# A state-space layer on chunks of four frames, with its matrices and tables built during the first MLP

## The reference, cut to what matters

```python
def s5_grouped(u, ...):          # 128 groups of 16 channels, 64 complex states in each
    step = exp(log_step)[:, None]
    lam_bar = exp(lam * step)
    b_bar = ((lam_bar - 1.0) / lam)[:, :, None] * b
    bu = einsum('blgh,gph->blgp', uf, b_bar)
    _, h = associative_scan(combine, (lam_bar, bu), axis=1)   # h_t = lam_bar * h_{t-1} + bu_t
    y = real(einsum('blgp,ghp->blgh', h, c)) + d_skip * uf
...
    y = s5_grouped(rmsnorm(x, mix_norm_o), ...)
    val, gate = split(gelu(y) @ w_glu)
    x = x + val * sigmoid(gate)
    x = x + square(relu(rmsnorm(x, ffn_norm[1]) @ w_up[1])) @ w_down[1]
```

## Time and profile before

| | |
|---|---|
| median of three runs | 2263.25 us (2261.49 to 2263.97) |
| profiled execution, first to last instruction | 2258.3 us |
| between the two | 4.95 us |
| busy share PE / DVE / ACT / POOL | 92% / 67% / 43% / 36% |
| mean granted TensorE clock | 0.952 |
| state-space stage | about 1090 to 1342 us |
| first MLP | about 370 to 1090 us |

### The profile page before, as it was taken

How to read it: one execution, slowest core, us unless ns; L and a number is a source line. 1 busy time by engine, 2 the same in 40 slices (tenths; PEclk the granted TensorE clock), 3 DMA queues, 4 the chain that set the end, 5 groups by cost and what they waited for, 6 DMA issues and landing times.

```text
span 2258.3 us, 38008 instructions
## 1 busy us (share of the span) xinstructions
PE 2073.3 (92%) x12259; PEld 1774.8 (79%) x12259; DVE 1513.1 (67%) x1828; ACT 971.4 (43%) x1347; POOL 814.3 (36%) x1249
## 2 busy tenths in 40 slices
PE   6969699999999999999565569999999999999998
PEld 5758588888888888888444458888888888888887
DVE  6887777755665665656799975657656655655653
ACT  3425544444444444434423324444444444444443
POOL 4187765777767777102366650100000000000000
PEclk9979899999999999999776779999999999999999
DMA  8534356666666666676211116565555555655653
GB/s 199 160 113 136 109 182 200 192 206 198 191 205 197 195 201 198 190 223 207 79 38 33 37 36 186 174 197 181 189 186 182 185 191 179 186 191 179 185 193 131
DMA packets 388147, 374.86 MB, mean 166 GB/s; under 512 B 34667, under 2 KB 385276, under 8 KB 387836
## 3 DMA queue, kind: packets, MB, share of 16 engines
q1 hardware_dynamic: 384796, 363.51, 51.9%
q0 software_dynamic: 3104, 10.49, 1.5%
q10 hardware_dynamic: 192, 0.14, 0.0%
HBM read 361.38 MB, written 12.58 MB: 166 GB/s over the span
## 4 chain that ended last, share of the span: by engine, by line
PE 81%; DVE 13%; issue 3%; ACT 1%; SPq 1%; DMA 1%; DVEq 1%; POOL 0%; ACTq 0%
PE ps L514 53%; PE ps L516 26%; DVE gb L1502 3%; DVE ab L1492 1%; DVE Wl L1103 1%; DVE ctm L1477 1%; DVE A L1133 1%; DVE uc L1456 1%; DVE A L1522 1%; DVE du L1468 1%; ACT Wh L817 1%; SPq L446 0%; DVE us L329 0%; PE px L586 0%; DMA xin<-in_x_dram 0%
## 5 line engine op out<-in xcount | busy, mean ns | idle before, releaser
L514 PE MATMUL ps<-A,Wh 128*128 128x512 f32 x5280 | 1857.2, 401 | 27.9 <-DVE A L1412 19.1
L516 PE MATMUL ps<-A,Wl 128*128 128x256 f32 x5280 | 1432.8, 282 | 0.0
L1103 DVE TENSOR_TENSOR Wl<-raw,Wh 128x1024 fp32r<-128x1024 f32 x660 | 828.5, 1268 | 579.2 <-ACT Wh L817 570.6
L514 PEld LDWEIGHTS ps<-A,Wh 128*128 128x128 f32 x5280 | 975.7, 189 | 248.3 <-issue 22.1
L817 ACT ACTIVATE Wh<-raw 128x1024 fp32r<-128x1024 f32 x660 | 689.6, 1057 | 808.4 <-PE ps L516 503.3
L516 PEld LDWEIGHTS ps<-A,Wl 128*128 128x128 f32 x5280 | 1001.5, 190 | 32.2
L1601 POOL TENSOR_TENSOR sq<-xT 128x512 f32 (+1 forms) x32 | 40.4, 1264 | 359.6 <-DVE xT L1181 177.4
L742 PE MATMUL ps<-hb,cst 128*32 128x128 f32 x128 | 36.7, 384 | 99.5 <-POOL hb L1723 99.5
L1665 POOL TENSOR_TENSOR ttmp<-ctab 128x4 f32<-128x4 f32 (+6 forms) x224 | 120.5, 538 | 17.6
L1666 POOL TENSOR_TENSOR ctab<-ttmp 128x2 f32<-128x2 f32 (+6 forms) x224 | 119.5, 534 | 17.6
L963 ACT ACTIVATE A<-cross 128x512 f32 (+1 forms) x64 | 40.4, 632 | 197.7 <-DVE cross L1427 197.7
(11 more groups left out here) (260 smaller groups left out, 1247.2 us busy)
## 6 DMA issues: line engine op xcount, KB each, us to landing
raw<-in_w_up_dram SPq DMA_DIRECT2D x256, 512.0 KB, 3.9
raw<-in_w_down_dram SPq DMA_DIRECT2D x256, 512.0 KB, 3.4
raw<-in_w_glu_dram SPq DMA_DIRECT2D x64, 512.0 KB, 3.9
raw<-in_w_in_e_dram SPq DMA_DIRECT2D x52, 512.0 KB, 3.9
raw<-in_w_out_e_dram SPq DMA_DIRECT2D x32, 512.0 KB, 3.6
s_tables<-ctab POOLq DMA_DIRECT2D x32, 256.0 KB, 3.3
tab<-s_tables SPq DMA_DIRECT2D x32, 256.0 KB, 3.0
xin<-in_x_dram SPq DMA_DIRECT2D x2, 1024.0 KB, 6.4
```

The costliest lines, as they stand in the source:

```text
L514: wide = lambda: mm(ps[:, b + t, :], Wh[:, s, c, cols], A[:, k, :], start=(n == 0), stop=(n == KC - 1))
L516: half = lambda: mm(ps[:, b + t, 0:L], Wl[:, s, c, cols], A[:, k, 0:L], start=False, stop=False)
L1103: tt(Wl[:, s], raw[:, s], Wh[:, s].bitcast(F32), ALU.subtract).then_inc(lo_split, 1)
```

## The change

The state-space stage takes four frames at a time (`CT = 4`, `NC4 = 64` steps). For that each chunk needs larger matrices, which are now built in the two middle quarters of the first MLP, one chunk for every two pairs, by all engines together, are stored to memory as one block of 1 MB per chunk (`par_d`: input matrices, output matrices, direct matrices, cosines, sines and negated sines), and read back into four slots.

In the preparation PE, after each even pair of the two quarters, brings C and B into place (`s5_c_columns`, 4 matrix multiplications, `s5_b_rows`, 16), and after each odd pair forms the direct kernels (`s5_kernels`, 16); POOL forms the products with powers of `lam` and the tables, chunk by chunk; ACT and DVE copy from PSUM beside their weight splits. The two quarters and the stage are unrolled. POOL no longer makes `bbar` or tables anywhere else; the B and C matrices are loaded from the POOL queue after the first layer's mixer.

In the stage the input is scaled and put into memory by ACT during the last eight pairs (`u_d`) and read back with four frames on the partitions by POOL's queue; PE makes 16 small matrix multiplications for a chunk's scan input and 40 for its output, all of 64 x 64 tiles with 64 columns; DVE makes two products, one scan of 512 columns (decay, result in PSUM; a zero decay at each of the 8 segments' starts) and two products; POOL makes one subtraction for the turn, the input's scaling by the norm and the low part of the result; ACT fills the decay into PSUM, makes the gelu and the high part. The result goes through memory (`y_d`) to come back channel-major, by SP. The frames lie in another order within a chunk through the GLU, and the residual addition puts them back.

SP's program:

```diff
-            for k, s5_b in enumerate((s5_b_re, s5_b_im)):
-                sp.dma_start(braw[:, k], s5_b[0].rearrange("(j g) p h -> (g p) j h", g=2)).then_inc(b_loaded, 16)
...
-            sp.wait_ge(bbar_stored, 32)
-            sp.dma_start(bch[:, :, :], bbar_d.rearrange("c p f -> p c f")).then_inc(bc_loaded, 16)
-            for k, s5_c in enumerate((s5_c_re, s5_c_im)):
...
-            sp.wait_ge(tab_stored, KC * 32)
-            for c in range(2):
-                load_tables(c, c)
...
+            def load_slot(c):
+
+                if c >= NSLOT:
+                    sp.wait_ge(s5_y, c - NSLOT + 1)
+                sp.dma_start(slot[:, c % NSLOT, :], par_d[c]).then_inc(slot_loaded[c % NSLOT], 16)
+
+            sp.wait_ge(kd_stored, 16)
+            for j in range(2, 8):
+                load_pair(g + 8 + j, w_down[0], (QTR - 1) * D, j * TW)
+                if j - 2 < NSLOT:
+                    load_slot(j - 2)
...
+            for c in range(KC):
+                sp.wait_ge(s5_ge, c + 1)
+                sp.dma_start(y_d[c].rearrange("(t q) (j n) -> (q j) t n", t=TPC, j=CT), yb[:, c % 2])\
+                    .then_inc(y_stored[c % 2], 16)
+                if c + NSLOT < KC:
+                    load_slot(c + NSLOT)
+                sp.wait_ge(y_stored[c % 2], 16 * (c // 2 + 1))
+                if c >= 3:
+                    sp.wait_ge(a2_ready, 48 + c - 2)
+                sp.dma_start(yt[:, c % 3, :], y_d[c]).then_inc(y_loaded[c % 3], 16)
```

PE in the first MLP, then in the stage (`s5_out` waits for `s5_p` of its chunk):

```diff
+                if hook:
+                    for q in range(1, QTR - 1):
+                        for j in range(8):
+                            up(j, j % 2, q, False)
+                            hook((q - 1) * 16 + j)
+                        for j in range(8):
+                            down(j, j % 2, q)
+                            hook((q - 1) * 16 + 8 + j)
...
+            def s5_b_rows(c):
+
+                pe.wait_ge(bp_ready, c + 1)
...
+            def prepare(n):
+
+                if n % 2 == 0:
+                    s5_c_columns(n // 2)
+                    s5_b_rows(n // 2)
+                else:
+                    s5_kernels(n // 2)
...
+            s5_in(0)
+            s5_in(1)
+            for c in range(KC):
+                s5_out(c)
+                if c + 2 < KC:
+                    s5_in(c + 2)
```

DVE in the stage:

```diff
+            def s5_rotate(c):
+
+                dve.wait_ge(s5_v, c + 1)
+                if c >= 2:
+                    dve.wait_ge(s5_z, c - 1)
+                tt(ab[:, c % 2, 0], v_bank(c), cos_of(c), ALU.mult)
+                tt(ab[:, c % 2, 1], v_bank(c), sin_of(c), ALU.mult).then_inc(s5_rot, 1)
+
+            def s5_scan(c):
+
+                dve.wait_ge(s5_z, c + 1)
+                dve.wait_ge(s5_rho, c + 1)
+                nc.vector.tensor_tensor_scan(ps[:, 2 + c % 2, :], ps[:, c % 2, :], zb[:, c % 2].rearrange("p t k n -> p (t k n)"),
+                                             0.0, ALU.mult, ALU.add).then_inc(s5_g, 1)
...
+                tt(pp[:, c % 2, 0, :, :, 1:NC4 + 1], g_bank(c), cos_of(c), ALU.mult)
+                tt(pp[:, c % 2, 1, :, :, 1:NC4 + 1], g_bank(c), sin_of(c), ALU.mult).then_inc(s5_p, 1)
+
+            s5_rotate(0)
+            dve.wait_ge(pp_zero, 1)
+            for c in range(KC):
+                if c + 1 < KC:
+                    s5_rotate(c + 1)
+                s5_scan(c)
```

POOL in the first MLP:

```diff
+            def turns(c):
...
+                while n < NC4:
...
+                    link(tt(tmp[0][:, :, 0:n], c0, ct_, ALU.mult))
+                    link(tt(tmp[1][:, :, 0:n], s0, st_, ALU.mult))
+                    link(tt(tmp[2][:, :, 0:n], s0, ct_, ALU.mult))
+                    link(tt(tmp[3][:, :, 0:n], c0, st_, ALU.mult))
+                    tt(cos[:, :, n:2 * n], tmp[0][:, :, 0:n], tmp[1][:, :, 0:n], ALU.subtract)
+                    link(tt(sin[:, :, 0, n:2 * n], tmp[2][:, :, 0:n], tmp[3][:, :, 0:n], ALU.add))
+                    n *= 2
...
+            for c in range(KC):
+                b_powers(c)
+                turns(c)
+                c_powers(c)
+                store(c)
```

More of the change, by code:

```diff
@@ L767, in _, with s5_in @@
-            s5_prepare(0, 0)
-            s5_direct(0, 0)
-            s5_prepare(1, 1)
+            mlp(P_MLP0, 8, 2, 16, 2, hook=prepare)
+            def s5_in(c):
+                pe.wait_ge(us_ready, c + 1)
+                pe.wait_ge(slot_loaded[c % NSLOT], 16 * (c // NSLOT + 1))
+                if c >= 2:
+                    pe.wait_ge(s5_rot, c - 1)
+                for t in range(TPC):
+                    for k in range(2):
+                        for g in range(2):
+                            own = slice(64 * g, 64 * g + 64)
+                            n = S_IN + (2 * t + k) * HD
+                            last = mm(v_bank(c)[own, t, k, :], slot[own, c % NSLOT, n:n + HD], us2[own, c % 4, t, :],
+                                      start=True, stop=True)
+                last.then_inc(s5_v, 1)
@@ new lines, in s5_out @@
+            def s5_out(c):
+                pe.wait_ge(s5_p, c + 1)
+                if c >= 2:
+                    pe.wait_ge(s5_ge, c - 1)
+                direct = slot[:, c % NSLOT, S_DIR:S_COS].rearrange("p (t n) -> p t n", t=TPC)
+                for t in range(TPC):
+                    for g in range(2):
+                        own = slice(64 * g, 64 * g + 64)
+                        mm(y_bank(c)[own, t, :], direct[own, t], us2[own, c % 4, t, :], start=True, stop=False)
+                    for k, w, m in ((0, 0, 0), (0, 1, 1), (1, 1, 0), (1, 0, 1)):
+                        for g in range(2):
+                            own = slice(64 * g, 64 * g + 64)
+                            n = S_OUT + (2 * t + k) * HD
+                            last = mm(y_bank(c)[own, t, :], slot[own, c % NSLOT, n:n + HD], pp[own, c % 2, w, t, m, 0:NC4],
+                                      start=False, stop=((k, m) == (1, 1)))
+                last.then_inc(s5_y, 1)
@@ L1069, in _ @@
+            for c in range(KC - 3, KC):
+                s5_high(c)
             act.preload_act_table(ACT.Sigmoid)
@@ new lines, in _ @@
+            mlp(P_MLP0, False, prepare)
+            rms()
+            for j in range(CT):
+                frames = rs.rearrange("p (n j) -> p j n", j=CT)[:, j]
+                if j == 0:
+                    link(ts(rss[:, :], frames, jm[:, 0:1], None, ALU.mult))
+                else:
+                    last = stt(rss[:, :], frames, jm[:, j:j + 1], rss[:, :], ALU.mult, ALU.add)
+                    if j < CT - 1:
+                        link(last)
+            last.then_inc(rss_ready, 1)
@@ new lines, in power, with weight @@
+            def power(i):
+                return [lamp[:, k, :, i - 1] for k in range(2)]
+            def weight(j):
+                return [ep[:, k, :, j] for k in range(2)]
+            pool.wait_ge(s5_small, 1)
+            for k in range(2):
+                link(nc.gpsimd.tensor_copy(power(1)[k], lam[:, k, :]))
+                link(nc.gpsimd.tensor_copy(weight(CT - 1)[k], coef[:, k, :]))
+            product(*power(2), power(1), power(1))
+            product(*power(3), power(2), power(1))
```

785 lines of the change are left out of this document (369 added, 416 removed).

## The result

| | before | after |
|---|---|---|
| median, five runs each | 2263.25 us (2259.87 to 2265.88) | 2271.48 us (2269.60 to 2274.82) |
| ratio after to before | | 1.0043, 95% interval 1.0031 to 1.0056 |
| profiled execution | 2258.3 us | 2272.7 us |

The changed kernel is slower, as forecast, but by 8 us and not by 58: 2271.5 us where 2321 was forecast. It lies inside the range.

The account below looks back on a forecast made before the run. PE matrix multiplications bound most of the kernel, the state-space stage excepted. Preparation +144, stage -72, attention -8 and weights -6 sum to +58 us: span 2316, median 2321 us, range 2235 to 2390 us.

Parts of the forecast that it names:

- POOL sets the pace from the second chunk on: MLP preparation, S being the second quarter's start: POOL's 32.7 us per chunk exceeds PE's 25.1, adding 144 us.
- take 32.7: Preparation: POOL's time per chunk in us, its own work plus collisions with eight VectorE subtractions; ends 30.5 and 35.5.
- 23.0: Preparation: POOL's undisturbed time per chunk in us, for 52 instructions and a DMA.
- 1.2 us for each of them: Preparation: time POOL loses to each VectorE weight subtraction, eight per chunk, read from today's half chunk.
- PE waiting some 7 us per chunk.: Second and third MLP quarters: PE waits for a POOL sum ahead of the hook's 16 multiplications, 14 times.
- period 4.0 + 6.0 + 0.2 = 10.2: State-space stage: microseconds per chunk, DVE 4.0 and PE 6.0 in series plus 0.2 for semaphores; today 14.9.
- 15 periods, 153: State-space stage: 153 us between a 19.5 us start and 7.0 us end; stage 179.5 instead of 251, -72.
- Full clock in the stage's bursts: Rival, state-space stage: PE takes 4 us per chunk, period 8.2 us; +28, 2291 us; chance 0.16.
- The small multiplications don't overlap: Rival, state-space stage: period 14.8 us, the stage's gain is gone; +130, 2393 us; chance 0.12.
- POOL keeps up: Rival, preparation: POOL's chunk takes at most 25.1 us, PE pays only its hooks; -46, 2217 us; chance 0.15.
- A new transfer wait: Rival: crowded DMA engines or a late `kd_stored` cost +20 to +40, about 2350 us; chance 0.05.
- The product from PSUM ... bears the page out.: Stage: two products at 1.29 us taken to support the skill page: DVE with one SBUF input doesn't contend with POOL.

Follow-up runs that it names:

- input-first order: In the stage of the changed kernel, PE makes chunk c+2's scan input ahead of chunk c's output instead of behind it; 2220.14 us.
- The filler: Changed kernel plus ten unread 128-column PE multiplications ahead of each stage chunk's output, keeping PE busy; 2245.27 us.

## Why the prediction was right in its sign and wrong in its size

Of the 43.6 us between forecast and measured span, the preparation and the stage have 21 each, and the attention 3; the weights take 1 back.

- **POOL sets the pace from the second chunk on.** Right, and shown by leaving its turns out. `bp_ready` of chunk 1 came at S + 32.5 us (forecast S + 34), of chunk 15 at S + 467.4 (forecast S + 492). The term that was mis-sized is "take 32.7": it measured 31.07, and 14 x 1.63 = 22.8 us. With the 1.5 us of chunk 1 that makes 24.3 us too much; 3.3 of them came back behind chunk 15, where two pairs with the last hooks took 28.4 us, 5.8 over the pairs alone, and I had allowed 2.5. Inside the 32.7, "23.0" was 24.2 and "1.2 us for each of them" was 0.86. I had put the whole difference of one half chunk, 7.9 us, down to its 6.6 subtractions; what is left without them (24.2 against 23.0) shows that a part of it belonged elsewhere. To what stays open.
- **"PE waiting some 7 us per chunk."** It waited 61.0 / 14 = 4.4 us, while the cycle was 31.07 - 25.3 = 5.8 us longer than PE's own. The rest, 1.4 us, goes with a lower clock: 0.94 in 550 to 950 us, where the run without turns, which has no wait, has 1.00. It cost nothing more, since POOL sets the pace, but it makes the wait look smaller than the loss.
- **Hooks, 2.5 us a chunk.** 2.7 measured.
- **POOL's tail.** 58 us after chunk 15, forecast 70, and no wait for it: right.
- **The stage, "period 4.0 + 6.0 + 0.2 = 10.2".** Right in its mechanism, at half clock: 9.93 to 10.1 us. Wrong in three places of the sum. "15 periods, 153": there are 14, since the last scan has no rotate ahead of it and follows after 2.46 us; this alone is 10.2 - 2.5 = 7.7 us, an error of counting that the program's order would have shown. The mean period is (1345.60 - 1213.99) / 14 = 9.40 us, mostly because part of each four chunks runs at the higher clock: 14 x 0.8 = 11.2 us. (By its own numbers the price of a multiplication is 0.42 / 2 / 2 = 0.105 and not 0.107 us, which is 0.1 us per period.) The start was 17.0 us instead of 19.5, the end 7.7 instead of 7.0. Together 158.7 us instead of 179.5.
- **"Full clock in the stage's bursts"** was a rival with 8.2 us. It came true for a part of the chunks; I should have taken a share of it into the sum, since the mean of 0.68 in the earlier trace rows was already a mixture of the two levels.
- **"The small multiplications don't overlap"** is refuted: 0.199 us apiece when they can't, 0.109 as written. *POOL keeps up* is refuted by the 61.0 us of waiting. *A new transfer wait* cost nothing: ACT waits once for weights, 3.30 us at 1055.70 us, where the 2 MB of direct matrices have just been stored, and the difference between the two kernels stays within 0.2 us there; `bp` and VectorE are what PE waits for in the two stretches, PE what VectorE waits for in the stage (82.5 us).
- **The attention, -8.** -11.0, all from the old `bbar`. **The weights, -6.** -4.9. At the same place of the changed kernel ACT waits for PE, not for a transfer.
- **"The product from PSUM ... bears the page out."** True, but not by the row that I gave: at 1227.24 us POOL was idle. The same two products at 1233.08 us, with POOL's L1722 and L1723 at work, take 1.29 us as well.

Not settled: how much of the gain of the input-first order is the order and how much the clock that comes with it. The filler changes the clock alone (-26 us), the order changes both (-51 us).

## What to carry to other kernels

Work that is hidden beside a stretch has a pace: compare its cycle on each engine, collisions included, with the main engine's, and spread it until the slower one fits; here 52 small instructions with two pairs for a chunk cost 79 us more than PE's own share, and the same with three pairs nothing. In a loop that hands a chunk back and forth between two engines, put ahead whatever doesn't need the other's answer, and count the periods by the order of the program, the first and last included. Where PE waits within a period, its lower clock lengthens its own half as well, so a removed wait can give back more than itself: 4.4 us of waiting in a chunk of the preparation were 5.8 us of time.

## What the runs showed of the hardware

- The 64 x 64 multiplications of 64 columns in float32: 0.109 us each on two alternating diagonal tiles at half clock, 0.199 on one tile at half clock, 2.4 / 40 = 0.06 on two at full clock.
- PE with a wait of 3.85 us in each period of 9.4 was granted 0.70 of the clock; with the wait filled down to 1.42 us it was granted 1.00.
- A VectorE and a POOL instruction, both with two SBUF inputs: the one that began first kept its time (the scan 1.22 us), the other took 2.11 us instead of 1.26; in the kernel before, where POOL began first, it was the scan that took 0.88 instead of 0.39. Against a stream of 1.27 us subtractions POOL lost 0.86 us for each.
